# A two-block transformer kernel: first mixer's attention turned by row halves, weighed partly by GpSimd, one pair later

## The reference, cut to what matters

```python
mix = nsa_attention(h, a_w_in, a_b_gate, a_pe_k, a_w1_k, a_w2_k,
                    a_pe_v, a_w1_v, a_w2_v, a_w_out, rel_bias)
x = x + mix
x = x + swiglu(rmsnorm(x, norm_ffn[0]), ffn_w_up[0], ffn_w_down[0])
```

## Time and profile before

| | us |
|---|---|
| median of 3 runs (lowest, highest) | 1298.45 (1298.41, 1301.5) |
| the profiled execution's own time | 1297.85 |
| its span in the trace | 1296.1 |
| TensorE busy | 1266.3 (98%) |
| VectorE busy | 812.3 (63%) |
| ScalarE busy | 641.7 (50%) |
| GpSimd busy | 275.7 (21%) |
| granted TensorE clock in all 40 slices of the span | 9 tenths or more of full speed |

### The profile page before, as it was taken

The page is one execution under the profiler, slowest core; times in us unless marked ns, Lnnn a source line. Parts: engine busy times, 40 slices in busy tenths (PEclk is TensorE's granted clock), DMA queues, the critical chain, the costliest instruction groups (busy, mean ns, idle before and its releaser), DMA issues.

```text
span 1296.1 us, 19580 instructions
## 1 busy us (share of the span) xinstructions
PE 1266.3 (98%) x7427; PEld 1058.7 (82%) x7427; DVE 812.3 (63%) x1194; ACT 641.7 (50%) x932; POOL 275.7 (21%) x362
## 2 busy tenths in 40 slices
PE   9999999999999999999999999999999999999997
PEld 7986788888799987888888788888887778888886
DVE  4568665555574476654656755656789876755554
ACT  4439554444453365543444644445544683534442
POOL 6520210000000041103000589602276210200000
PEclk9999999999999999999999999999999999999999
DMA  9960655555455645467655555654545346555651
GB/s 303 268 130 20 179 163 194 193 182 182 155 195 183 175 116 161 166 194 175 215 189 163 189 181 185 224 194 135 191 130 163 130 130 195 191 184 193 194 189 38
DMA packets 155996, 224.79 MB, mean 173 GB/s; under 512 B 13507, under 2 KB 108091, under 8 KB 155932
## 3 DMA queue, kind: packets, MB, share of 16 engines
q1 hardware_dynamic: 145248, 212.55, 51.7%
q0 software_dynamic: 10064, 10.54, 4.2%
q10 hardware_dynamic: 620, 0.83, 0.2%
HBM read 222.56 MB, written 1.25 MB: 173 GB/s over the span
## 4 chain that ended last, share of the span: by engine, by line
PE 82%; DVE 8%; ACT 4%; POOL 2%; DMA 2%; issue 2%; DVEq 0%; SPq 0%; POOLq 0%; ACTq 0%
PE bank L223 24%; PE bank L225 23%; PE bank L224 23%; PE bank L244 5%; DVE units_lo L178 2%; PE bank L232 2%; PE bank L747 1%; DMA raw_units<-in_ffn_w_up 1%; ACT arena L1584 1%; PE bank L1000 1%; DVE arena L3092 1%; PE bank L239 1%; POOL rows L1261 1%; DVE arena L3083 1%; DVE arena L2545 1%
## 5 line engine op out<-in xcount | busy, mean ns | idle before, releaser
L666 DVE TENSOR_TENSOR units_lo<-raw_units,units_hi 128x2048 fp32r<-128x2048 f32 x96 | 223.0, 2322 | 154.3 <-ACT units_hi L620 154.3
L223 PE MATMUL bank<-units_hi,turned_hi 128*128 128x512 f32 (+1 forms) x792 | 307.1, 388 | 3.0 <-DVE units_lo L178 1.3
L225 PE MATMUL bank<-units_hi,turned_lo 128*128 128x512 f32 (+1 forms) x792 | 302.1, 381 | 0.0
L224 PE MATMUL bank<-units_lo,turned_hi 128*128 128x512 f32 (+1 forms) x792 | 301.7, 381 | 0.0
L178 DVE TENSOR_TENSOR units_lo<-raw_units,units_hi 128x2048 fp32r<-128x2048 f32 (+2 forms) x101 | 228.3, 2268 | 96.0 <-ACT units_hi L170 95.6
L170 ACT ACTIVATE units_hi<-raw_units 128x2048 fp32r<-128x2048 f32 (+2 forms) x101 | 189.5, 1885 | 100.2 <-PE bank L225 76.8
L620 ACT ACTIVATE units_hi<-raw_units 128x2048 fp32r<-128x2048 f32 x96 | 183.5, 1911 | 103.9 <-PE bank L225 95.6
L223 PE MATMUL bank<-units_hi,second_hi 128*128 128x512 f32 (+1 forms) x560 | 218.7, 391 | 0.0
L225 PE MATMUL bank<-units_hi,second_lo 128*128 128x512 f32 (+1 forms) x560 | 216.5, 387 | 0.0
L224 PE MATMUL bank<-units_lo,second_hi 128*128 128x512 f32 (+1 forms) x560 | 216.4, 386 | 0.0
L223 PEld LDWEIGHTS bank<-units_hi,turned_hi 128*128 128x128 f32 x792 | 149.0, 188 | 32.8 <-DVE units_lo L178 3.0
(11 more groups left out here) (373 smaller groups left out, 1778.2 us busy)
## 6 DMA issues: line engine op xcount, KB each, us to landing
raw_units<-in_ffn_w_up SPq DMA_DIRECT2D x88, 512.0 KB, 4.7
raw_units<-in_ffn_w_in SPq DMA_DIRECT2D x88, 512.0 KB, 4.6
raw_units<-in_ffn_w_down SPq DMA_DIRECT2D x22, 1024.0 KB, 5.0
raw_units<-in_ffn_w_out SPq DMA_DIRECT2D x22, 1024.0 KB, 4.9
raw_units<-in_w_in SPq DMA_DIRECT2D x18, 1024.0 KB, 5.1
raw_units<-in_b_w_q SPq DMA_DIRECT2D x12, 1024.0 KB, 5.2
raw_units<-in_a_w_in SPq DMA_DIRECT2D x9, 1024.0 KB, 11.9
raw_units<-in_kv_w SPq DMA_DIRECT2D x6, 1024.0 KB, 5.3
```

Of the source, the lines that this page charges most:

```text
L223: pe.matmul(out, lh, rh, start=start, stop=False, skip_group_check=True)
L224: pe.matmul(out, lh, rl, start=False, stop=False, skip_group_check=True)
L225: return pe.matmul(out, ll, rh, start=False, stop=True, skip_group_check=True)
L666: dve.tensor_tensor(m.WL[:, slot(n0 + j), :], m.RAW[:, slot(n0 + j), :], m.WH[:, slot(n0 + j), :].bitcast(F32), ALU.subtract).then_inc(m.l ...
```

## The change

The weights of a pair are turned by row halves: bank 4 receives rows 0 to 63 of both heads, bank 5 rows 64 to 127. It takes 12 transposes of 64 rows in place of 6 of 128. ScalarE copies bank 4 and VectorE copies bank 5. The sums read the new layout of `A.PT` through a strided view. For pairs 2 to 13 GpSimd multiplies three of the four parts by their factors (`GPSIMD_PARTS`, 256, 128 and 128 columns), and VectorE one of 256 columns. These pairs are turned in step i+3 and summed in step i+4; pairs 0, 1, 14 and 15 stay at i+2 and i+3. The ring `A.PB` holds four pairs.

```diff
-RING_PAIRS = 3
-TURN_AFTER, SUM_AFTER = 2, 3
+RING_PAIRS = 4
+WEIGHED_BY_GPSIMD = range(2, 14)
+TURN_AT = [i + 2 + (i in WEIGHED_BY_GPSIMD) for i in range(NPA)]
+SUM_AT = [t + 1 for t in TURN_AT]
...
+def turn_pair_a_tensor(pe, m, i):
+
+    if i >= 1:
+        pe.wait_ge(m.s("a_turned_copied"), 2 * i)
+    for par in range(2):
+        wait_weighted_a(pe, m, i, par)
+        for b, at in enumerate((S, 0, P)):
+            for half in range(2):
+                rows = slice(half * DH, (half + 1) * DH)
+                to = (par * 3 + b) * DH
+                ins = pe.transpose(m.pb[4 + half][:, to:to + DH], m.A.PB[rows, i % RING_PAIRS, par, at:at + P],
+                                   m.IDENT[rows, rows])
+                if (par, b) == (1, 2):
+                    ins.then_inc(m.s("a_turned"), 1)
...
 def attend_a_tensor(pe, m):
     pe.wait_ge(m.s("a_left_out"), 5)
-    for p in range(2, NPA + SUM_AFTER):
+    for p in range(2, SUM_AT[-1] + 1):
         if p < NPA:
             score_pair_a_tensor(pe, m, p)
         if p == 2:
             pe.wait_ge(m.s("a_right_out"), 5)
...
+        for i in range(NPA):
+            if TURN_AT[i] == p:
+                turn_pair_a_tensor(pe, m, i)
+        for i in range(NPA):
+            if SUM_AT[i] == p:
+                sum_pair_a_tensor(pe, m, i)
...
 def bias_pair_a_vector(dve, m, p):
     T, G, r, br = pair_a(p)
+    if p >= RING_PAIRS:
+        dve.wait_ge(m.s("a_turned"), 2 * (p - RING_PAIRS) + 2)
...
+PARTS_A = [(par, *half) for par in range(2) for half in HALVES_A]
+GPSIMD_PARTS, VECTOR_PARTS = (0, 1, 3), (2,)
+
+
+def weigh_part_a(eng, m, i, x):
+
+    par, a, b, tok = PARTS_A[x]
+    w = m.A.PB[:, i % RING_PAIRS, par, a:b]
+    return eng.tensor_scalar(w, w, m.A.RD[:, i, par, tok:tok + 1], None, ALU.mult)
+
+
+def weigh_pair_a_vector(dve, m, i):
+    factor_pair_a_vector(dve, m, i)
     dve.wait_ge(m.s("a_factor"), 2 * i + 2)
...
+    for x in VECTOR_PARTS if i in WEIGHED_BY_GPSIMD else range(4):
+        weigh_part_a(dve, m, i, x).then_inc(m.s("a_weighted"), 1)
+
+
+def attend_a_gpsimd(pool, m):
+
+    for i in WEIGHED_BY_GPSIMD:
+        pool.wait_ge(m.s("a_factor"), 2 * i + 2)
+        for x in GPSIMD_PARTS:
+            weigh_part_a(pool, m, i, x).then_inc(m.s("a_weighted_by_gpsimd"), 1)
+
+
+def turned_pair_a_vector(dve, m, i):
+
+    dve.wait_ge(m.s("a_turned"), 2 * i + 2)
+    if i >= 2:
+        dve.wait_ge(m.s("a_summed"), 2 * (i - 1))
+    dve.tensor_copy(m.A.PT[:, i % 2, 1, :], m.pb[5][:, 0:3 * P])\
+        .then_inc(m.s("a_turned_copied"), 1)
...
@@ attend_a_vector
         if 2 < p < NPA + 1:
             weigh_pair_a_vector(dve, m, p - 1)
+        for i in range(NPA):
+            if TURN_AT[i] == p:
+                turned_pair_a_vector(dve, m, i)
...
@@ attend_a_scalar
-            for par in range(2):
-                act.wait_ge(m.s("a_turned"), 2 * i + par + 1)
+        for i in range(NPA):
+            if TURN_AT[i] == p:
+                act.wait_ge(m.s("a_turned"), 2 * i + 1)
                 if i >= 2:
                     act.wait_ge(m.s("a_summed"), 2 * (i - 1))
-                act.activation(m.A.PT[:, i % 2, par, :], m.pb[4 + par][:, 0:3 * P], ACT.Copy)\
+                act.activation(m.A.PT[:, i % 2, 0, :], m.pb[4][:, 0:3 * P], ACT.Copy)\
                     .then_inc(m.s("a_turned_copied"), 1)
...
             compress_gpsimd(pool, m)
+            attend_a_gpsimd(pool, m)
             pool.wait_ge(m.s("a_biased"), 4 * NPA)
```

More of the change, by code:

```diff
@@ L1476, in score_pair_a_tensor, with wait_weighted_a @@
                 ins.then_inc(m.s("a_scored"), 1)
+def wait_weighted_a(pe, m, i, par):
+    first, n = WEIGHED_BY_GPSIMD[0], len(WEIGHED_BY_GPSIMD)
+    if i in WEIGHED_BY_GPSIMD:
+        if par == 1:
+            pe.wait_ge(m.s("a_weighted"), 4 * first + i - first + 1)
+        pe.wait_ge(m.s("a_weighted_by_gpsimd"), 3 * (i - first) + 2 + par)
+    else:
+        pe.wait_ge(m.s("a_weighted"), (4 * i if i < first else 4 * (i - n) + n) + 2 * par + 2)
+def turn_pair_a_tensor(pe, m, i):
[11 more added lines that the diff above has]
+                    ins.then_inc(m.s("a_turned"), 1)
@@ new lines, in sum_pair_a_tensor @@
+def sum_pair_a_tensor(pe, m, i):
+    T, G, r, br = pair_a(i)
+    out = m.pb[6 + T % 2]
+    if i == 0:
+        pe.wait_ge(m.s("cmp_ready"), TT)
+    if br == 0:
+        if T >= 2:
+            pe.wait_ge(m.s("a_out_lo"), T - 1)
+        rr = slice(32 * r, 32 * r + 32)
+        for par in range(2):
+            g = 2 * G + par
+            pe.matmul(out[par * DH:(par + 1) * DH, 0:S], m.A.VCR[rr, g, :], m.A.PCT[rr, g, :], start=True,
+                      stop=False, skip_group_check=True, tile_position=(32 * r, par * DH))
+    pe.wait_ge(m.s("a_turned_copied"), 2 * (i + 1))
+    v = (m.A.VS, m.A.VW)[br]
+    for keys, (a, b) in enumerate(((0, S), (P, S))):
+        for par in range(2):
+            g = 2 * G + par
+            blocks = slice(0, 2) if keys == 0 else slice(2, 3)
+            pt = m.A.PT[:, i % 2, :, :].rearrange("p h (x b q) -> p h x b q", x=2, b=3)[:, :, par, blocks, :]\
+                .rearrange("p h b q -> p b h q")
+            ins = mm(pe, out[par * DH:(par + 1) * DH, a:b].rearrange("p (b h q) -> p b h q", h=2, q=DH),
+                     v[:, keys, g * DH:(g + 1) * DH], pt, False, keys == 1 and br == 1)
+            if keys == 1:
+                ins.then_inc(m.s("a_summed"), 1)
@@ L1485, in attend_a_tensor @@
             pe.wait_ge(m.s("a_right_out"), 5)
-        if TURN_AFTER <= p < NPA + TURN_AFTER:
-            i = p - TURN_AFTER
-            for par in range(2):
[L1489 to L1520, removed]
+        for i in range(NPA):
[4 more added lines that the diff above has]
+                sum_pair_a_tensor(pe, m, i)
 def bias_pair_a_vector(dve, m, p):
     T, G, r, br = pair_a(p)
+    if p >= RING_PAIRS:
+        dve.wait_ge(m.s("a_turned"), 2 * (p - RING_PAIRS) + 2)
     for par in range(2):
@@ L1527, in bias_pair_a_vector @@
         dve.wait_ge(m.s("a_scored"), 2 * p + par + 1)
-        if p >= RING_PAIRS:
-            dve.wait_ge(m.s("a_turned"), 2 * (p - RING_PAIRS) + par + 1)
         for a, b, tok in HALVES_A:
@@ L1535, in bias_pair_a_vector, with factor_pair_a_vector @@
                                      accum_out=m.A.NM[:, p, par, tok:tok + 1]).then_inc(m.s("a_biased"), 1)
-def weigh_pair_a_vector(dve, m, i):
+def factor_pair_a_vector(dve, m, i):
     T, G, r, br = pair_a(i)
@@ L1545, in weigh_pair_a_vector @@
     dve.tensor_tensor(m.A.RD[:, i, :, :], m.A.RD[:, i, :, :], g, ALU.mult).then_inc(m.s("a_factor"), 1)
-    dve.wait_ge(m.s("a_factor"), 2 * i + 2)
[L1547 to L1551, removed]
+PARTS_A = [(par, *half) for par in range(2) for half in HALVES_A]
[6 more added lines that the diff above has]
+    factor_pair_a_vector(dve, m, i)
+    dve.wait_ge(m.s("a_factor"), 2 * i + 2)
+    for x in VECTOR_PARTS if i in WEIGHED_BY_GPSIMD else range(4):
[11 more added lines that the diff above has]
+        .then_inc(m.s("a_turned_copied"), 1)
 def attend_a_vector(dve, m):
-    for p in range(2, NPA + 3):
+    for p in range(2, SUM_AT[-1] + 1):
         if p < NPA:
@@ L1559, in attend_a_vector @@
             weigh_pair_a_vector(dve, m, p - 1)
+        for i in range(NPA):
+            if TURN_AT[i] == p:
+                turned_pair_a_vector(dve, m, i)
         for T in range(7):
-            if LAST_PAIR[T] + 4 == p:
+            if SUM_AT[LAST_PAIR[T]] + 1 == p:
                 out_lo(dve, m, "a", T, T, m.pb[6 + T % 2][:, 0:S])
```

## The result

| | before | after |
|---|---|---|
| median of 5 runs each, us (lowest, highest) | 1298.45 (1297.74, 1301.98) | 1307.41 (1305.81, 1309.34) |
| ratio, 95% interval | | 1.0063 [1.0053, 1.0074] |
| span of the profiled execution, us | 1296.1 | 1305.6 |
| score 2 to the projection's first matmul, us | 94.42 to 141.29: 46.87 | 94.39 to 149.55: 55.16 |

The change makes the kernel 9.0 us slower. I had forecast +1.0 and a range that ends at 1303.0. The attention of pairs 2 to 15, from the start of score 2 to the start of the projection's first matmul, accounts for 8.29 us (55.16 - 46.87) of the 9.5 us by which the spans differ.

A forecast was written before the change was run, and what follows sets the result against it. No engine full; a two-step attention chain through TensorE and ScalarE sets the pace. 2.5 us gained, 3.9 lost in the tail, 0.4 taken off: +1.0, median 1299.4 us; range 1294.9 to 1303.0.

The forecast's parts named there:

- In the attention's steady stretch the clock is full: Opening reading of the old trace's attention: clock full, TensorE busy 5.59 of 6.01 us, no engine full.
- signs of being wrong: Last score not earlier by 2 us, tail under 9 us, or VectorE's product or factor stretched or delayed.
- The walk: Attention summed score to score: 2.5 us gained up to score 15, 3.9 lost from there to the projection, 1.4 slower.
- take off 0.4: Correction to the attention sum: the same additions over the old order ended at 141.9 against the trace's 141.3.
- The loop: Two-step attention cycle through score, bias, exp, copy, turn and sum that sets the pace: from 6.01 to 5.68 us.
- 1.37 us a pair: GpSimd's weighing of three parts: 0.62 for 256 columns plus 2 x 0.375 for 128 columns.
- 1.9 at most: GpSimd's weighing of a pair including a 0.15 us start and at most one VectorE product of 0.365.
- the bound of 2.84: GpSimd's weighing stays hidden while a pair takes less than half a two-step cycle, 2.84 us.
- A: Rival: attention's tail as short as before, 2.5 us or more gained, 1295 to 1296 us; chance 0.20.
- B: Rival: ScalarE runs ahead, TensorE alone bounds at 4.94 us per two steps, 1295.7, or 1294 with short tail; chance 0.06.
- C: Rival: VectorE stands still 0.62 us a pair behind GpSimd's 256-column part and becomes the bound, 1302.9 us; chance 0.10.
- D: Rival: GpSimd's weighing takes 3.3 us a pair and sets the attention's pace, 5.5 us slower, 1304; chance 0.06.

The follow-up runs named there:

- warm_both: The changed kernel plus identity matmuls, results never read, in TensorE's waits ahead of turns 1, 3, 13, 14 and 15: 1301.47 us, ratio 1.0017.
- full_turns: The changed kernel with six full 128x128 transposes a turn instead of twelve halves, the rest as changed: 1309.65 us, ratio 1.0079.
- halves_only: The changed kernel with VectorE weighing all parts and no turn late; half transposes, split copies and ring of four kept: 1303.03 us, ratio 1.0033.
- warm_tail: The changed kernel plus identity matmuls, results never read, ahead of turns 13, 14 and 15 only: 1302.05 us, ratio 1.0026.
- two_parts: The changed kernel with GpSimd weighing only the two 128-column parts, pairs 2 to 15 all turned a step later, no extra matmuls: 1302.08 us, ratio 1.0028.
- warm_start: The changed kernel plus identity matmuls, results never read, ahead of turns 1 and 3 only: 1306.26 us, ratio 1.0055.
- before_stalls: The kernel before the change with three extra ScalarE copies ahead of each of copies 12, 13 and 14: 1302.52 us, ratio 1.0026.
- lag_all_busy: The changed kernel with pairs 2 to 15 all turned late and weighed by GpSimd, extra matmuls ahead of turns 1, 3, 13, 14, 15: 1300.99 us, ratio 1.0015.

## Why the prediction was wrong

**The step that failed** is in the first part: "In the attention's steady stretch the clock is full". That is what the earlier trace rows show of the kernel before; I carried it over to a kernel in which TensorE waits longer, and priced its waits at their length alone. What the runs showed in its place is a clock that falls to 0.50 behind such waits. "TensorE waiting ahead of turns 13, 14 and 15 for some 1.5 to 2, 1.2 and 0.8 us" was right (2.13, 1.19, 0.76). That the work behind such waits may run at half the clock had no term in the sum and no rival. It costs 6.56 us in the attention (55.16 in the change, 48.60 with the waits filled). Behind it the projection starts at 0.50 as well, from 149.55 to about 151, some 0.7 us of the 1.2 that the attention leaves over; the remaining 0.5 was not traced.

One of the prediction's own signs of being wrong came true by it: the last score is not earlier by 2 us but later by 0.24 (39.39 us behind score 2, 39.15 before), since the first fall takes 2.38.

**The walk was right in its size.** At full clock (`warm_both`) the attention is 1.73 us longer; my sum gave 1.4, and 1.0 after I "take off 0.4" for an overestimate that did not appear. Of the 1.73 some 0.3 may be the fillers' own. The pieces: 2.14 us gained up to score 15 (walked 2.5), the tail 11.59 us (walked 11.55). "The tail takes 11.55 us, 3.9 more" measured 3.87.

**The loop.** It takes 5.73 to 5.80 us for the 5.68 forecast, with the half transposes at 0.46 and 0.52 for 0.47 and 0.56. With the old form the loop of `full_turns` is 6.01.

**GpSimd was mis-sized**: "1.37 us a pair" measured 2.27, more than the "1.9 at most" that had its start in it. I took the price from a row of another instruction and from a product with two inputs; its 256-column part takes 1086 ns and its 128-column parts 604. It is not waiting for VectorE that makes them long: the three parts that begin at 103.46 us take 2.25 us together, as the others do, though VectorE stands idle from 103.8 to 105.9. Why the row at 375 ns was quicker is open. GpSimd stayed under the bound of 2.84, so it ended no wait of TensorE; `halves_only` shows what GpSimd is for (6.14 against 5.73).

**The rivals.** A fell: the tail is not short. B fell: TensorE still waits for ScalarE's copy, 0.64 to 0.96 us in each loop. C fell: VectorE's product begins first (118.52 us, GpSimd's parts at 118.58) and takes 370 ns beside a working GpSimd. D had the direction of GpSimd's price but not its size. Its time, 1304, and C's, 1302.9, are nearer to the result than mine by luck, for reasons that are not the kernel's.

**What is shown and what is open.** Shown: filling the waits takes the falls away, each where it is filled, and with them 6.56 us; waits alone, put into the kernel before, cost their own length. Open: what decides whether a wait is followed by a fall, and how long the fall lasts. The profiled executions, with the waits nearest ahead:

| | waits, us | clock 0.50 from | for, us |
|---|---|---|---|
| the change, start | 1.71 | 99.9 | 6.8 |
| warm_tail, start | 1.71 | 99.4 | 3.4 |
| halves_only, start | 1.71 | none | |
| two_parts, start | 1.68 | none | |
| two_parts, turn 3 | 1.84 | 107.7 | 3.4 |
| the change, tail | 2.13 | 137.4 | 13.7 |
| warm_start, tail | 2.12, 1.42 | 139.2 | 10.2 |
| full_turns, tail | 1.68, 1.14 | 144.9 | 13.7 |
| halves_only, tail | 0.99, 0.98 | 139.6 | 6.8 |
| two_parts, tail | 1.72 | none | |
| before_stalls, tail | 1.54, 1.63, 0.63 | none | |

The length of the waits does not sort them. Nor does the idle time in the stretch ahead: `before_stalls` kept the clock with TensorE idle for 2.62 us of 135 to 140, and `halves_only` lost it in that stretch, with TensorE idle for 1.97. And one kernel, `two_parts`, differs from execution to execution. The Trainium skill's page "TensorE: Matmul & The Clock Gate", section "Part 1: The HAM clock gate", states that the gate watches how busy TensorE has been and runs free of the kernel, so that the same kernel changes clock at other points from run to run. The runs agree as far as they go: the same instructions fell at 99.9 us for 6.8 us in the change and at 99.4 for 3.4 in `warm_tail`. That this is what sorts the rows of the table is not shown, and whether it matters what TensorE did ahead of a wait, transposes or products, was not tried.

## What to carry to other kernels

When an edit lengthens or gathers TensorE's waits, price them twice: at their length, and as a rival in which the matmuls behind them run at the half clock, here 6.6 us where the new order itself costs 1.7. Look at the granted clock by stretch before the waits themselves, and if it falls, fill the waits with idle matmuls: that tells what the order costs and what the clock does. Look whether a filler stands in place of a wait, since one that does not costs its own time (1.30 us in `lag_all_busy`), and compare the changed part from start to start, since a fall elsewhere can move the whole time by more than the change. A price for GpSimd is taken from the same operation at the same width or given a wide bound: from its nearest row it was off by 1.7 times.

## What was not expected of the hardware

- The clock fell to 0.50 behind waits of 1.71 us (turn 1) and 2.13 us (turn 13), and stayed there for 6.8 and 13.7 us, although TensorE was full (5.00 of 5.00 us) in the stretches 100 to 105 and 145 to 150. In `halves_only` it fell behind waits of 0.99 and 0.98 us.
- The same instructions had a fall of 6.8 us in one execution and of 3.4 us in another (the change and `warm_tail`, near 100 us).
- Extra matmuls on the engine that bounds the kernel made it faster: 1307.41 to 1301.47 us, and 1302.08 to 1298.79 in `two_parts`.
- GpSimd's multiplication by a column of factors took 604 ns for 128 columns and 1086 for 256, against 375 for the 128-column instruction in the earlier trace rows.
